# Expert gate and up of a slot as one moving operand of 512 columns, and a shorter routing

## What is computed

```python
def hierarchical_moe(h, w_rg, b_rg, w_re, b_re, w1, w3, w2):      # h: 256 tokens x 1024
    p_group = softmax(t @ w_rg + b_rg)                             # 4 groups
    g_val, g_idx = lax.top_k(p_group, 1)                           # one group for each token
    fine = (t @ w_re + b_re).reshape(-1, 4, 4)                     # 4 experts in each group
    e_val, e_idx = lax.top_k(softmax(fine of that group), 2)       # two experts of the group
    combine = one_hot(group) * (weights of the two experts) * g_val
    for e in range(16):
        y_e = (silu(t @ w1[e]) * (t @ w3[e])) @ w2[e]              # 1024 -> 512 -> 1024
        out = out + combine[:, e:e + 1] * y_e
```

## Time and profile before

| | us |
|---|---|
| runs of the kernel (median of 3) | 2798.98 |
| lowest, highest | 2796.22, 2808.4 |
| the profiled execution | 2799.47 |
| its span, first to last instruction | 2797.6 |
| PE busy, of the span | 2672.2 (96%) |
| DVE busy | 1689.5 (60%) |
| ACT busy | 1211.8 (43%) |
| mean granted TensorE clock | 0.982 of full |

### The profile page before, as it was taken

The page is one execution under the profiler, slowest core; times in us unless marked ns, Lnnn a source line. Parts: engine busy times, 40 slices in busy tenths (PEclk is TensorE's granted clock), DMA queues, the critical chain, the costliest instruction groups (busy, mean ns, idle before and its releaser), DMA issues.

```text
span 2797.6 us, 38576 instructions
## 1 busy us (share of the span) xinstructions
PE 2672.2 (96%) x14019; PEld 2138.1 (76%) x14019; DVE 1689.5 (60%) x2562; ACT 1211.8 (43%) x1985; POOL 249.2 (9%) x378
## 2 busy tenths in 40 slices
PE   6999999999998999999999999999997899799999
PEld 5887588888774888887768888876885544699988
DVE  5764576776463766763356676655664451577676
ACT  4444444544332544443244454444442221466664
POOL 0001100100110001000110010011002000000000
PEclk9999999999998999999999999999998989899999
DMA  8542455554241554552355545435443211477784
GB/s 298 180 142 95 177 188 182 186 180 163 90 166 47 194 195 165 186 197 105 121 188 189 197 162 185 160 113 188 180 139 118 91 61 67 181 268 269 275 299 168
DMA packets 328512, 472.42 MB, mean 169 GB/s; under 512 B 8944, under 2 KB 266352, under 8 KB 328416
## 3 DMA queue, kind: packets, MB, share of 16 engines
q1 hardware_dynamic: 325120, 462.93, 46.2%
q0 software_dynamic: 2800, 8.04, 1.0%
q10 hardware_dynamic: 496, 0.17, 0.0%
HBM read 470.01 MB, written 1.10 MB: 168 GB/s over the span
## 4 chain that ended last, share of the span: by engine, by line
PE 87%; DVE 6%; ACT 3%; DMA 2%; POOL 1%; issue 1%; ACTq 0%; SPq 0%; DVEq 0%; POOLq 0%
PE psum_all L1222 23%; PE psum_all L1223 12%; PE psum_all L1334 6%; PE psum_all L1261 6%; PE psum_all L1262 5%; PE psum_all L1263 5%; PE psum_all L1410 4%; PE psum_all L1849 3%; PE psum_all L2761 2%; PE psum_all L2762 2%; PE psum_all L2763 2%; PE psum_all L1337 2%; DMA raw_ring<-in_w 1%; PE psum_all L1355 1%; PE psum_all L1374 1%
## 5 line engine op out<-in xcount | busy, mean ns | idle before, releaser
L1222 PE MATMUL psum_all<-hT_both,gu_hi 128*128 128x512 f32 x2816 | 1006.0, 400 | 16.7 <-DVE gu_lo L1065 10.4
L1223 PE MATMUL psum_all<-hT_both,gu_lo 128*128 128x256 f32 x2816 | 790.9, 281 | 0.0
L1222 PEld LDWEIGHTS psum_all<-hT_both,gu_hi 128*128 128x128 f32 x2816 | 530.1, 188 | 149.0 <-DVE gu_lo L1065 11.1
L1223 PEld LDWEIGHTS psum_all<-hT_both,gu_lo 128*128 128x128 f32 x2816 | 532.9, 189 | 6.2
L1065 DVE TENSOR_TENSOR gu_lo<-raw_ring,gu_hi 128x2048 fp32r<-128x2048 f32 x176 | 403.0, 2292 | 15.4 <-ACT gu_hi L1053 15.2
L1053 ACT ACTIVATE gu_hi<-raw_ring 128x2048 fp32r (+1 forms) x176 | 334.3, 1902 | 16.1 <-DVE oT L1546 12.2
L1091 ACT ACTIVATE cross_terms<-psum_all 128x256 f32<-128x256 f32 x176 | 67.4, 383 | 594.9 <-PE psum_all L1223 594.9
L1072 DVE TENSOR_TENSOR down_lo<-raw_ring,down_hi 128x1024 fp32r<-128x1024 f32 x240 | 292.4, 1218 | 24.1 <-ACT down_hi L1060 23.2
L1261 PE MATMUL psum_all<-down_hi,hidden_hi 128*128 128x512 f32 x704 | 277.3, 394 | 11.1 <-DVE hidden_lo L1158 10.4
L1262 PE MATMUL psum_all<-down_lo,hidden_hi 128*128 128x512 f32 x704 | 276.0, 392 | 0.0
L1263 PE MATMUL psum_all<-down_hi,hidden_lo 128*128 128x512 f32 x704 | 274.1, 389 | 0.0
(11 more groups left out here) (374 smaller groups left out, 3831.4 us busy)
## 6 DMA issues: line engine op xcount, KB each, us to landing
raw_ring<-in_ffn_w_in SPq DMA_DIRECT2D x176, 1024.0 KB, 7.0
raw_ring<-in_w SPq DMA_DIRECT2D x96, 1024.0 KB, 7.6
raw_ring<-in_ffn_w_out SPq DMA_DIRECT2D x88, 1024.0 KB, 9.1
raw_ring<-in_c_w_in SPq DMA_DIRECT2D x12, 768.0 KB, 5.4
raw_ring<-in_w_in SPq DMA_DIRECT2D x10, 768.0 KB, 5.4
gain<-in_norm_g POOLq DMA_DIRECT2D x12, 512.0 KB, 4.0
raw_ring<-in_a_w_in SPq DMA_DIRECT2D x8, 768.0 KB, 5.1
raw_ring<-in_b_w_in SPq DMA_DIRECT2D x8, 768.0 KB, 5.0
```

Of the source, the lines that this page charges most:

```text
L1222: nc.tensor.matmul(out, w_hi, K.hT_both[:, k, :, :].rearrange("p c s -> p (c s)"), start=k == 0, stop=False)
L1223: return nc.tensor.matmul(out[:, 0:SEQ], w_lo, K.hT_hi[:, k, :], start=False, stop=k == KT - 1)
```

## The change

Each half of a slot's split now holds four of the eight row tiles `k` with all 256 gate and 256 up columns, instead of all eight row tiles with half the columns. Gate and up of a row tile form one moving operand of 512 columns: a unit takes 24 products of 512 columns instead of 48 of 256. In the routing the fillers ahead of and behind the transposes go, the router's products run by row tile as `hT` comes, the counts are one product of 8 columns (and one for the running counts, with its own semaphore) instead of five, DVE adds the halves in two more small operations, and fillers stand in two new places (5 and 6, on another PSUM bank). SP loads one group number before the first transfer and each other one when first needed. ACT and DVE do the splits of the first slot between the small gathered tiles, ahead of tiles 2 and 5; PE starts the experts when two of the small tiles are split. The small gathered tiles take PSUM banks in another order.

```diff
-        self.ge_hi = at("e_gate_up_hi", [P, 2, KT, 2, P], self.arena + 8 * KT * SEQ, F32R)
+        self.ge_hi = at("e_gate_up_hi", [P, 2, KT // 2, 2, PAIR], self.arena + 8 * KT * SEQ, F32R)
...
-            group = [sp.value_load(K.gid[0:1, p:p + 1], min_val=0, max_val=3) for p in range(4)]
+            group = {}
             for s in b["slots"]:
                 n, h = n0 + s["n"], s["h"]
+                if s["pos"] not in group:
+                    at = s["pos"]
+                    group[at] = sp.value_load(K.gid[0:1, at:at + 1], min_val=0, max_val=3)
...
+E_KEEP = (5, 6)
...
-    return K.psum[:, (4 + k) % 8, 0:3 * P]
+    return K.psum[:, (6, 7, 4, 5, 0, 1, 2, 3)[k], 0:3 * P]
...
 def pe_route(K, pe, b):
-    keep_clock(K, KEEP_LAST)
...
-    keep_clock(K, KEEP_TURN)
     pe.wait_ge(K.sem.e_small, E_LOADS)
-    pe.wait_ge(K.sem.e_turn_act, 4)
-    pe.wait_ge(K.sem.e_turn_dve, 4)
-    for a in range(NT):
-        for k in range(KT):
+    for k in range(KT):
+        if k < 4:
+            pe.wait_ge(K.sem.e_turn_act, k + 1)
+        else:
+            pe.wait_ge(K.sem.e_turn_dve, k - 3)
+        for a in range(NT):
...
+    keep_clock(K, E_KEEP[0], 1)
     pe.wait_ge(K.sem.e_group, 1)
-    nc.tensor.matmul(K.psum[:, 6, 0:4], every, hot[0], start=True, stop=False)
-    nc.tensor.matmul(K.psum[:, 6, 0:4], every, hot[1], start=False, stop=True)
-    nc.tensor.matmul(K.psum[:, 6, 4:8], K.upto[:, :], hot[0], start=True, stop=True)
-    nc.tensor.matmul(K.psum[:, 6, 8:12], every, hot[0], start=True, stop=False)
-    nc.tensor.matmul(K.psum[:, 6, 8:12], K.upto[:, :], hot[1], start=False, stop=True).then_inc(K.sem.e_count, 1)
+    hot = K.r4[:, 0, :, :].rearrange("p a g -> p (a g)")
+    nc.tensor.matmul(K.psum[:, 4, 0:8], K.one.to_broadcast([P, P]), hot, start=True, stop=True).then_inc(K.sem.e_count, 1)
+    nc.tensor.matmul(K.psum[:, 3, 0:8], K.upto[:, :], hot, start=True, stop=True).then_inc(K.sem.e_upto_ps, 1)
+    keep_clock(K, E_KEEP[1], 1)
     pe.wait_ge(K.sem.e_place, NT)
...
 def act_route(K, act, b):
     for k in range(KT):
+        if k in (2, 5):
+            act_hi_expert(K, act, b, 0, k // 3)
         act.wait_ge(K.sem.e_gather, KT + k + 1)
...
 def dve_route(K, dve, b):
-    link(nc.vector.scalar_tensor_tensor(out=key, in0=K.psum[:, 6, 0:4], scalar=4.0, in1=K.eidx[:, 0:4],
+    link(nc.vector.scalar_tensor_tensor(out=key, in0=K.psum[:, 4, 0:4], scalar=4.0, in1=K.eidx[:, 0:4],
+                                        op0=ALU.mult, op1=ALU.add))
+    link(nc.vector.scalar_tensor_tensor(out=key, in0=K.psum[:, 4, 4:8], scalar=4.0, in1=key,
                                         op0=ALU.mult, op1=ALU.add))
...
+    dve.wait_ge(K.sem.e_upto_ps, 1)
...
+    link(nc.vector.tensor_tensor(tmp[:, 1, :], tmp[:, 1, :], K.psum[:, 4, 0:4], ALU.add))
...
     for k in range(KT):
+        if k in (2, 5):
+            dve_lo_expert(K, dve, b, 0, k // 3)
         dve.wait_ge(K.sem.e_h_hi, KT + k + 1)
...
-    for t in range(2):
-        dve_lo_expert(K, dve, b, 0, t)
...
 def raw_expert(K, b, n, t):
-    return raw_gu(K, (b["fill0"] + n) % RING, t).rearrange("p (g k) f -> p g k f", g=2)
+    r = K.raw[:, (b["fill0"] + n) % RING, 0:2 * KT * PAIR].rearrange("p (g k f) -> p g k f", g=2, k=KT)
+    return r[:, :, t * KT // 2:(t + 1) * KT // 2, :]
...
 def gate_up_bank(K, u):
-    bank = K.psum[:, 6 + u % 2, :].rearrange("p (t g f) -> p t g f", t=2, g=2)
-    return bank[:, :, 0, :], bank[:, :, 1, :]
+    return K.psum[:, 6 + u % 2, 0:PAIR], K.psum[:, 6 + u % 2, PAIR:]
...
-        out = K.psum[:, 6 + u % 2, t * SEQ:(t + 1) * SEQ]
-        for k in range(KT):
+        out = K.psum[:, 6 + u % 2, :]
+        for k in range(t * KT // 2, (t + 1) * KT // 2):
             h_hi, h_lo = tokens(x["T"], k)
-            w_hi, w_lo = (w[:, t, k, :, :].rearrange("p g f -> p (g f)") for w in (K.ge_hi, K.ge_lo))
+            w_hi, w_lo = (w[:, t, k % (KT // 2), :, :].rearrange("p g f -> p (g f)") for w in (K.ge_hi, K.ge_lo))
...
-    pe.wait_ge(K.sem.e_h_lo, KT)
+    pe.wait_ge(K.sem.e_h_lo, KT + 2)
```

More of the change, by code:

```diff
@@ L234, in __init__ @@
             some("e_group e_count e_order e_place e_gather")
+        self.e_upto_ps, = some("e_upto_ps")
         self.e_h_hi, self.e_h_lo, self.e_weights_ps, self.e_weights, self.e_rows, self.e_back = \
@@ L388, in map_memory @@
         self.dec = at("h_decay", [P, 2, 4, SEQ], o + 8 * 4 * SEQ)
-        self.ge_hi = at("e_gate_up_hi", [P, 2, KT, 2, P], self.arena + 8 * KT * SEQ, F32R)
-        self.ge_lo = at("e_gate_up_lo", [P, 2, KT, 2, P], self.arena + 16 * KT * SEQ, F32R)
+        self.ge_hi = at("e_gate_up_hi", [P, 2, KT // 2, 2, PAIR], self.arena + 8 * KT * SEQ, F32R)
+        self.ge_lo = at("e_gate_up_lo", [P, 2, KT // 2, 2, PAIR], self.arena + 16 * KT * SEQ, F32R)
         self.hS_hi = at("e_tokens_hi", [P, 3, KT, P], self.arena_end, F32R)
@@ L993, with keep_clock @@
 KEEP_LAST, KEEP_TURN, KEEP_MIX = 5, 1, 17
-def keep_clock(K, count):
+E_KEEP = (5, 6)
+def keep_clock(K, count, bank=7):
     for _ in range(count):
-        K.nc.tensor.matmul(K.psum[:, 7, SEQ:2 * SEQ], K.ident, K.cst[:, 0:SEQ], start=True, stop=True)
+        K.nc.tensor.matmul(K.psum[:, bank, SEQ:2 * SEQ], K.ident, K.cst[:, 0:SEQ], start=True, stop=True)
 def pe_turn_x(K, pe, b, h):
@@ L2424, in pe_route @@
                     ins.then_inc(K.sem.x_tr, 1)
-    keep_clock(K, KEEP_TURN)
     pe.wait_ge(K.sem.e_small, E_LOADS)
-    pe.wait_ge(K.sem.e_turn_act, 4)
-    pe.wait_ge(K.sem.e_turn_dve, 4)
-    for a in range(NT):
-        for k in range(KT):
-            ins = nc.tensor.matmul(K.psum[:, 7, a * 20:(a + 1) * 20], K.hT[:, k, a * P:(a + 1) * P], K.rw[:, k, :],
+    for k in range(KT):
[4 more added lines that the diff above has]
+        for a in range(NT):
+            ins = nc.tensor.matmul(K.psum[:, 7 - a, 0:20], K.hT[:, k, a * P:(a + 1) * P], K.rw[:, k, :],
                                    start=k == 0, stop=k == KT - 1)
     ins.then_inc(K.sem.e_lg, 1)
+    keep_clock(K, E_KEEP[0], 1)
     pe.wait_ge(K.sem.e_group, 1)
-    hot = [K.r4[:, 0, a, :] for a in range(NT)]
-    every = K.one.to_broadcast([P, P])
-    nc.tensor.matmul(K.psum[:, 6, 0:4], every, hot[0], start=True, stop=False)
-    nc.tensor.matmul(K.psum[:, 6, 0:4], every, hot[1], start=False, stop=True)
-    nc.tensor.matmul(K.psum[:, 6, 4:8], K.upto[:, :], hot[0], start=True, stop=True)
-    nc.tensor.matmul(K.psum[:, 6, 8:12], every, hot[0], start=True, stop=False)
-    nc.tensor.matmul(K.psum[:, 6, 8:12], K.upto[:, :], hot[1], start=False, stop=True).then_inc(K.sem.e_count, 1)
+    hot = K.r4[:, 0, :, :].rearrange("p a g -> p (a g)")
+    nc.tensor.matmul(K.psum[:, 4, 0:8], K.one.to_broadcast([P, P]), hot, start=True, stop=True).then_inc(K.sem.e_count, 1)
+    nc.tensor.matmul(K.psum[:, 3, 0:8], K.upto[:, :], hot, start=True, stop=True).then_inc(K.sem.e_upto_ps, 1)
+    keep_clock(K, E_KEEP[1], 1)
     pe.wait_ge(K.sem.e_place, NT)
@@ L2493, in dve_route @@
     for a in range(NT):
-        link(nc.vector.scalar_tensor_tensor(out=K.lg[:, a, :], in0=K.psum[:, 7, a * 20:(a + 1) * 20],
+        link(nc.vector.scalar_tensor_tensor(out=K.lg[:, a, :], in0=K.psum[:, 7 - a, 0:20],
                                             scalar=K.st[:, PRE_R + a:PRE_R + a + 1], in1=K.rb[:, :],
@@ L2647, in y_high @@
                 .then_inc(K.sem.e_y_hi, 1)
-    for t in range(2):
-        act_hi_expert(K, act, b, 0, t)
     act.wait_ge(K.sem.e_arg, 1)
@@ L2668, in act_experts @@
         gate, _ = gate_up_bank(K, u)
-        nc.scalar.activation(K.sg[:, u % 2, :].rearrange("p (t f) -> p t f", t=2), gate, ACT.Silu,
+        nc.scalar.activation(K.sg[:, u % 2, :], gate, ACT.Silu,
                              scale=K.ws[:, x["T"], 4:5]).then_inc(K.sem.silu, 1)
@@ L2724, in dve_experts @@
         _, up = gate_up_bank(K, u)
-        nc.vector.scalar_tensor_tensor(out=K.hid[:, u % 2, :].rearrange("p (t f) -> p t f", t=2), in0=up,
+        nc.vector.scalar_tensor_tensor(out=K.hid[:, u % 2, :], in0=up,
                                        scalar=K.ws[:, x["T"], x["e"]:x["e"] + 1],
-                                       in1=K.sg[:, u % 2, :].rearrange("p (t f) -> p t f", t=2),
+                                       in1=K.sg[:, u % 2, :],
                                        op0=ALU.mult, op1=ALU.mult).then_inc(K.sem.hid_done, 1)
```

2 lines of the change are left out of this document (1 added, 1 removed).

## The result

| | median us | runs |
|---|---|---|
| before | 2805.03 | 6 (2796.22 to 2810.54) |
| changed | 2787.36 | 6 (2781.93 to 2793.58) |
| ratio | 0.9942 | 95% interval 0.9922 to 0.9962 |

The changed kernel is 0.58% faster, which is clear of no change, and the bound of 0.5% lies inside the interval.

The account below looks back on a forecast made before the run. PE was taken to bound the kernel, holding 87% of the chain that ended last. The experts' net -7.3 us and the start's -8.3 summed to -15.6, so 2798.98 became 2783.4 us, range 2777 to 2792.

Parts of the forecast that it names:

- The pitch: Experts' gate and up: 24 products at 0.229 us replace 48 at 0.120, 0.25 us less a unit, 9.5 over 38 units.
- The refills: Ring slots refilled in the experts: PE stalls at six places, each losing 0.375 us of the gain, 2.2 us in all.
- parts 1 and 2: Experts' 38 units: the shorter pitch less what ring-slot refills take back, net -7.3 us, from -4.5 to -8.
- The gap formula: Skill page's isolated gap, columns over 2.4 plus 2.5 ns: 63 ns a unit, 2.5 us over the experts' stage.
- The start: Routing up to the second expert unit: row weights at 2420.2 instead of 2429.52; net -8.3 us, from -5 to -10.5.
- The clock allowance: Start of the experts: +1.0 us for a clock fall in PE's pauses, bounds 0 and +4.5.
- Those named for being right: Included units 8.48 us apart, row weights near 2420, first transfer near 2396.7, split-weight waits of 0.6 us at six places.
- the three named for being wrong: ACT waiting for a transfer at the first split, a pitch of 0.24, or clock 0.5 behind 2409.
- Refills bound the stage: Rival: late transfers at ring refills cut the experts' gain to -2 to -4 us; about 2788; chance 0.15.
- The start gives half: Rival: late weights, half-clock fillers or clock falls leave the start -4 us; time 2787.5 to 2788; chance 0.15.
- the pitch doesn't fall: Rival: experts' 512-column products cost 0.239 us, so the shorter pitch gives nothing; time 2790.7; chance 0.07.
- slower: Rival: clock stays at half behind the pauses, 4.8 us more a unit; 2813 from six units on; chance 0.03.

Follow-up runs that it names:

- The run with transfers by rows: Changed kernel with each slot's gate and up moved in four transfers instead of two, row tiles 0 to 3 first; timed ratio to before 0.9919.
- the run in pieces: Changed kernel with GpSimd's two subtractions for the low part of x cut into four instructions of 256 columns each; timed ratio to before 0.9909.
- the start alone: Changed kernel with the experts' products put back to 256 columns, keeping the new routing, first transfer and order of first splits; timed 0.29% faster than before.
- the pitch alone: Kernel before with only the experts' products changed (512 columns, halves by row tiles); timed 0.23% faster than before.

## Why the prediction was right, point by point

**The pitch** was right in kind and 0.05 us a unit too small: 8.41 instead of 8.71 is 0.30, not 0.25. The new pitch is that of `down`, and both came out a little under 0.229, (8.41 - 0.23) / 36 = 0.227. By the undisturbed pitch 38 units give 11.4 and not 9.5.

**The refills** were at five of the six places named, and the loop kept its length (14.85 against 14.83), as the prediction had it. But the cost was mis-sized. The excess of the unit intervals over an undisturbed unit is 0.55 + 0.48 + 0.45 + 1.72 + 0.49 + 0.69 = 4.4 us before and 1.08 + 1.08 + 1.54 + 4.06 + 1.02 = 8.8 after: 4.4 lost and not 2.2. Three causes show: each place loses three halves of 0.15 and not 0.125, the transfer in the loop took 8.06 and 9.11 us at two of them instead of 7.46 and 8.71 (at the last it was shorter, 7.54 instead of 8.20), and at the longest wait the clock fell, some 1.5 us (4.06 less the wait of 2.29 and the 0.3 of a restart). The net over the 38 units is -6.15 against the -7.3 of parts 1 and 2. Of the 0.85 that 11.4 - 4.4 leaves open, 0.5 lies in the last three intervals, which hold other products too and fell by 0.4 instead of 0.9, and 0.3 in units of 8.43 to 8.55. That the gain was put 1.9 too low and the loss 2.2 too low is luck for the sum: the two errors nearly cancel. The run with transfers by rows shows that all 8.8 hung on the transfer.

**The gap formula** of the Trainium skill (TensorE: Matmul & The Clock Gate, Back-to-back issue gap) would have made the pitch worth 2.5 us over the stage by the prediction's working, an estimate from that page. Exactly it gives 24 x 2.5 = 60 ns a unit, 2.3 us. The rows of `down` decided, and the trace after confirms them with 0.30 us a unit.

**The start**, put into before's time by the 6.22 us between the two R: count product 2393.8 (forecast 2393.6), first transfer 2396.9 (2396.7), gather 2398.4 (2398.4), first weights 2404.9 (2404.0), row weights 2420.0 (2420.2). Only the landing is off: 8.0 us behind the first issue and not 7.3, so that ACT waited 0.5 us for it. The 7.3 came from bytes over GB/s; in the trace before, up's transfer lands at 2410.6, 7.9 behind the first issue. That the group choice waits on GpSimd was right, and so was which operation is held by the second subtraction; the run in pieces shows it. The five new fillers behind the router were expected at full clock, 2.4 us; the clock had fallen and they took 4.1, which cost nothing, since they ended 0.8 ahead of the counts. Which of the many edits carry the start is now measured: one group load 1.6, fillers 1.45, order of the splits 2.8, of which 1.6 is the clock. They are not to be added, as each was taken from the whole alone, and the fewer counts and removed fillers were not tried by themselves.

**The clock allowance** was 1.0 us for the start. In the profile the clock cost 1.6 behind the row weights and fell again in the first `down`. The latter hardly shows: the first two transposes are 9.72 apart, against 9.46 to 9.51 in changed kernels without that fall, as there TensorE waits 1.1 us for split weights behind the `down`, and here it does not. In the stretch from the row weights to the first transpose alone, the other traces show anything from 0 to 3.3 us. An allowance can't catch that, and its size is the same as that of the effects looked for.

**The sum** of -15.6 stands against -13.8 in the profiled pair and -16 (0.58% of 2800) by the ratio. In the pair the way from R to the second transpose gave -7.6 (forecast -8.3) and the 38 units -6.15 (forecast -7.3), both inside their bounds. The range's lower end does not follow from these bounds: 2798.98 - 10.5 - 8 is 2780.5, and not 2778.

**The signs.** Those named for being right came, with units 8.41 apart and not 8.48, and waits of 0.7 to 2.3 us at five places, not 0.6 at six. But two of the three named for being wrong came too. ACT did wait for the transfer at the first split, and the clock was 0.5 behind 2409 in before's time, at the row weights and in the first `down`. The clock cost 1.6 us against the 1.0 allowed; the late landing did not move the row weights, which came where they were forecast.

**The rivals.** "Refills bound the stage" was partly true: 4.4 of 11.4 us, and not the half or more that this case gave. "The start gives half", "the pitch doesn't fall" and "slower" fell: by the start alone, by the pitch alone, and by every run.

## What to carry to other kernels

When a bound engine gets faster by a small step, look at loops beside it that are already level with it: here 14.83 us of release, transfer, split and use against 14.6 us of products. What the faster pitch gained was lost there, and cutting that loop (the first half's rows moved first) was worth 8.9 us of the stage, more than the pitch itself kept. Where a stage is split in two halves, choose the cut so that the transfer can be cut the same way. And where the clock moves, compare stages of two traces before whole times: the run in pieces looks faster by its ratio than the stage that it changed explains.

A filler is free only as long as what it fills is late. When the wait is shortened, the filler is next on the chain.

## What the runs showed of the hardware

- In these traces a GpSimd subtraction in the on-chip memory held a two-input VectorE operation to its end, however small the latter: 1.14 and 2.28 us for 8 columns, 0.65 at most when GpSimd's instructions were 0.71 long. VectorE got in between two pieces.
- The granted clock went to half during, or within 1 us behind, the 20 products of 5 columns in seven of the twelve traces, and not in the other five. With two fillers ahead of them, a pause of 0.3 us and the 27 us before at 1.00, it fell all the same (2420 to 2422 of that run, where TensorE was counted busy for 2.00 of 2.00 us). Which edits make it fall there can't be read from these runs.
- R lay at 2380.4 to 2392.1 us in the twelve profiled executions, 12 us apart, though nothing ahead of it was changed. The clock accounts for it: TensorE was at half clock for 71.7 to 95.6 us ahead of R, and R less half of that time is 2343.1 to 2344.5 in all twelve. Why it falls more often in one execution than in another stays open. The runs of one kernel spread by as much. A small change is better read from a fixed point in the trace than from spans.
